# A tile of small scalars is declared 8 columns wide in place of 16, and all that lies behind it in SBUF starts 32 bytes earlier

## The reference

```
first block:  h = rms_norm(x)*(1+scale)+shift ; split(h @ w_in)
              window attention with context keys  +  gated delta rule in 64-token chunks, both directions
              x += gate * ((sigmoid*attn + sigmoid*delta) @ w_out)
              x += gate * (square(relu(h2 @ w_mlp1)) @ w_mlp2)
second block, twice:
              u, q, k, v = split(modulate(rms_norm(x)) @ w_in2)
              centred means of u over 2, 4, 8, 16 tokens, each group through a 128x128 matrix (w_pool)
              differential attention over context + latent keys
              x += gate * (mix @ w_out2) ;  x += gate * (square(relu(h2 @ w_m1)) @ w_m2)
              (the context stream likewise, in the first of the two layers only)
final rms_norm
```

## The kernel before

| tile | start before | rest by 64 |
|---|---|---|
| raw | 16512 | 0 |
| ws | 65664 | 0 |
| hh | 90240 | 0 |
| xT | 123008 | 0 |
| rs | 149056 | 0 |
| sq | 151104 | 0 |
| mi | 155200 | 0 |
| ar, ar2, hc1, gg, g2 | 155264 | 0 |
| yy, gc2 | 188032 | 0 |
| hc2 | 204416 | 0 |
| ctx2 | 220800 | 0 |

## Time and profile before

### The profile page before, as it was taken

The page is one execution under the profiler, slowest core; times in us unless marked ns, Lnnn a source line. Parts: engine busy times, 40 slices in busy tenths (PEclk is TensorE's granted clock), DMA queues, the critical chain, the costliest instruction groups (busy, mean ns, idle before and its releaser), DMA issues.

```text
span 2666.4 us, 45804 instructions
## 1 busy us (share of the span) xinstructions
PE 2505.2 (94%) x19622; PEld 2041.3 (77%) x19622; DVE 1557.0 (58%) x2412; ACT 931.7 (35%) x1599; POOL 115.6 (4%) x222
## 2 busy tenths in 40 slices
PE   6999977779999999999998999999999998999997
PEld 3777666667887788887777888888887766788886
DVE  3355577766666788854675556645445466544444
ACT  3344443323235223342553432222233254423322
POOL 0000001111100001000000000000000000000000
PEclk8999999989999999999999999999999999999999
DMA  6000000004653555411002123333321101222210
GB/s 278 32 32 1 33 3 4 4 4 166 222 210 129 178 193 190 174 44 59 5 32 80 64 95 127 127 127 127 127 95 44 64 32 65 94 101 115 100 64 32
DMA packets 32202, 244.88 MB, mean 92 GB/s; under 512 B 3616, under 2 KB 3776, under 8 KB 20992
## 3 DMA queue, kind: packets, MB, share of 16 engines
q1 hardware_dynamic: 11808, 164.83, 15.5%
q0 software_dynamic: 20192, 77.11, 9.1%
HBM read 239.83 MB, written 2.10 MB: 91 GB/s over the span
## 4 chain that ended last, share of the span: by engine, by line
PE 85%; DVE 9%; issue 3%; ACT 2%; DMA 1%; POOL 0%; DVEq 0%; ACTq 0%; POOLq 0%
PE ps L337 56%; PE ps L2190 2%; PE ps L2419 2%; PE ps L949 1%; PE ps L2447 1%; PE ps L2463 1%; PE ps L1370 1%; PE ps L367 1%; PE ps L905 1%; PE ps L2465 1%; PE ps L2464 1%; PE ps L369 1%; PE ps L368 1%; PE ps L950 1%; PE ps L951 1%
## 5 line engine op out<-in xcount | busy, mean ns | idle before, releaser
L337 PE MATMUL ps<-hh,ws 128*128 128x512 f32 x3216 | 751.7, 393 | 11.2 <-DVE hh L524 7.5
L337 PEld LDWEIGHTS ps<-hh,ws 128*128 128x128 f32 x3216 | 601.2, 188 | 143.9 <-issue 15.6
L318 ACT ACTIVATE ws<-raw 128x1024 fp32r<-128x1024 f32 x295 | 308.7, 1049 | 423.9 <-PE ps L337 390.8
L326 DVE TENSOR_TENSOR ws<-raw,ws 128x1024 fp32r<-128x1024 f32 x295 | 359.7, 1221 | 156.4 <-ACT ws L318 156.4
L337 PE MATMUL ps<-g,ws 128*128 128x512 f32 x1536 | 355.3, 390 | 0.0
L337 PEld LDWEIGHTS ps<-g,ws 128*128 128x128 f32 x1536 | 286.4, 188 | 58.0
L337 PE MATMUL ps<-gg,ws 128*128 128x512 f32 x960 | 221.5, 391 | 2.1 <-ACT ws L318 2.1
L1807 DVE SCALAR_TENSOR_TENSOR xT<-ps,mods,xT 128x512 f32<-128x512 f32 x120 | 90.0, 750 | 213.6 <-PE ps L337 206.3
L337 PEld LDWEIGHTS ps<-gg,ws 128*128 128x128 f32 x960 | 181.2, 189 | 40.6 <-ACT ws L318 2.4
L1970 DVE TENSOR_TENSOR sq<-sq 128x512 f32<-128x512 f32 (+1 forms) x128 | 80.0, 625 | 142.9 <-ACT sq L1947 142.9
L1947 ACT ACTIVATE sq<-ps 128x512 f32<-128x512 f32 (+1 forms) x128 | 69.3, 542 | 258.3 <-PE ps L337 244.3
(11 more groups left out here) (378 smaller groups left out, 3571.4 us busy)
## 6 DMA issues: line engine op xcount, KB each, us to landing
raw<-in_w_m SPq DMA_DIRECT2D x32, 2048.0 KB, 7.8
raw<-in_w_ada POOLq DMA_DIRECT2D x80, 512.0 KB, 3.9
raw<-in_w_mlp SPq DMA_DIRECT2D x16, 2048.0 KB, 7.9
ar<-in_w_ada POOLq DMA_DIRECT2D x48, 512.0 KB, 3.9
raw<-in_w_in SPq DMA_DIRECT2D x8, 2048.0 KB, 7.7
raw<-in_w_mg SPq DMA_DIRECT2D x8, 1536.0 KB, 7.2
raw<-in_w_out SPq DMA_DIRECT2D x6, 2048.0 KB, 8.0
raw<-in_w SPq DMA_DIRECT2D x5, 2048.0 KB, 7.9
```

The lines of the kernel that those rows point to most:

```text
L318: e.activation(w_of(n)[0], pieces[n][2], ACT.Copy).then_inc(*hi(n))
L326: e.tensor_tensor(l, pieces[n][2], h.bitcast(F32), ALU.subtract).then_inc(*lo(n))
L337: m = e.matmul(o, a, b, start=n == 0, stop=n == 3 * kt - 1)
```

## The change

The tile `mi` gets 8 columns in place of 16, 32 bytes in place of 64. Nothing else in the file is different.

```
--- before.py
+++ after.py
@@ -132,7 +132,7 @@
         ones = sb("ones", [P, P])
         rs = sb("rs", [P, T])
         sq = sb("sq", [P, 2, T])
-        mi = sb("mi", [P, 16])
+        mi = sb("mi", [P, 8])
         REST = 18432
```

## The result

The changed kernel is slower: its median is 2681.56 us (2679.49 to 2684.59, four runs), that of before in the same comparison 2666.86 us. The ratio is 1.0054, 95% interval 1.0040 to 1.0068, so 14.4 us with 10.7 to 18.1. I had forecast no change and called a loss 27 in 100 likely; the loss lies inside my range of 2658 to 2700 us and outside the forecast's own range.

What follows compares the result with a forecast made beforehand. The prediction took TensorE's matmuls to bound the kernel. All terms were 0, so 2668.16 us stayed 2668.16, or 2665.5 us on the median's scale; the range was 2658 to 2700 us, the forecast's own 2661 to 2671.

Steps and rivals of the forecast that it cites:

- Which engine the time hangs on: Whole kernel: TensorE, busy 2505.2 of 2666.4 us and 85% of the chain, so whatever stretches matmuls moves the time.
- The exchange rate: 5040 matmuls reading the region: they sit on the path nearly one for one, 1 ns more each being 5.04 us.
- I take 0 ns for each matmul: fp32r matmuls whose moving operand lies in the region, mostly line 337: no cost from a start with a rest of 32.
- The bound of 1 ns: Same matmuls: flights of the float32 pool matmuls leave 1 ns either way, -5 to +5 us.
- The look at group 3 of line 2211: Check after the change: this float32 pool pair, then starting on a multiple of 64, should still take 1.02 us.
- The fp32r rival: Matmuls on the region: an uneven start needs one more 64-byte block, 6.7 ns each, 33.6 us, 2699 us; chance 0.17.
- half a block: Matmuls on the region: half the extra 64-byte block, 3.4 ns each, giving 2682 us.
- the small things: ScalarE's and VectorE's writes, small matmuls' weight loads and DMA: about 16 us in full, 2682 us, half likelier; chance 0.10.
- The faster rival: Weights and moving tile on the same rest hinder each other; 32 bytes apart saves 33 us, 2633 us; chance 0.11.
- VectorE, ScalarE and DMA: Their accesses to the region: 0 each; bounds of 2 us, about 2.5 us and 2.9 us.
- Weights loaded from the region: Some 2,600 small matmuls loading weights from hc and ar: 0, with at most 9 us up or down.
- The two rules: SBUF's 16-byte cachelines make a 32-byte shift free; DMA fetching from 256-byte boundaries gives ar's loads 131 beats, not 132.

Runs made afterwards that it cites:

- e2: Kernel before with 32 bytes put ahead of ws and 32 behind it, so ws starts with a rest of 32: 2692.42 us, ratio 1.0102.
- e6: Kernel before with only the second block's g2, gc2, hc2 and ctx2 moved 32 bytes later: 2671.96 us, ratio 1.0007.
- m4: New kernel with line 337's matmul pattern alone, in plain float32 and fp32r at other widths and distances; float32 at 512 columns, 32 bytes: 41.36 us.
- e1: Kernel before with a 32-byte tile put ahead of raw, so every large tile starts with a rest of 32: 2665.98 us, ratio 1.0005.
- e5: Changed kernel with 32-byte gaps putting g2, gc2, hc2 and ctx2 back where they were: 2673.34 us, ratio 1.0018 against before.
- m1: New kernel with line 337's matmuls alone, weights and moving tile at varied starts: 227.5 ns with both on 64, 233.5 with only the moving tile off.
- the sweep: New kernel with line 337's matmuls alone, moving operand at growing distances from one weights tile; 227 ns at multiples of 256 bytes, 512 columns.

## Why the prediction was wrong

*Which engine the time hangs on* was right. The exchange rate was, too, for the change and for e2: the busy time added on the big products (15.6 and 28 us) came out in the time (14.4 and 27). In e6 it did not quite.

*TensorE, fp32r: "I take 0 ns for each matmul"* is the step that failed. Measured: +6.7 ns at 512 columns in an uninterrupted stretch and about -1.3 ns at 256. In busy time `g` +9.1, `gg` +6.1, `yy` +1.3, line 2190 on `hc` +0.5, `hc` -0.4 and `gc` -1.0 are 15.6 us, against 14.4 us (10.7 to 18.1) in the runs. What decides is the distance in bytes between the weights and the moving operand: it was a multiple of 256 and is now 32 bytes off.

The 0 came from float32 rows, of which I had written that they run at half the rate and may hide what fp32r can't. m4 shows just that: float32 is flat to 0.1 ns a matmul at every distance. The bound of 1 ns that I drew from their flights, and with it the chance of 0.62, was therefore a bound on another instruction. The text named the weakness but gave the rival that rests on it no more than 0.17. The look at group 3 of line 2211 in the changed kernel could not have shown the effect either: `w_pool` lies in `ar2` as well, so the weights moved along with the latent means. Only its two context tiles in `raw` stayed, and these, whose distance to their weights did change by 32 bytes, kept their 380 ns, as float32 does in m4.

*The fp32r rival* gave 6.7 ns and foretold 233 ns on `g` beside 227 on `hh`, which is what the profile shows. Its mechanism was wrong nonetheless: it is no extra block, since e1, with every start on a rest of 32, is as fast as before. And at 256 columns it foretold 127 ns where 118.7 came. Its 33.6 us (33.8 with the rounded 6.7 ns) are 2688 matmuls at 512 columns x 6.7 = 18.0 us, of which 16.5 are there in busy time, and 2352 at 256 columns x 6.7 = 15.8 us, which aren't. The range held the measured time because it had been stretched to reach this rival, and the 2682 us that the prediction names twice, for half a block and for the small things, are near it by luck: neither is what happened.

*The faster rival* looked at the right quantity, where the weights and the moving operand lie relative to each other, with the wrong sign at 512 columns. It was taken for unlikely because the pool matmuls were no faster at another distance, and these were float32.

*VectorE, ScalarE and DMA* were each priced at 0 and stayed there: 692 and 742 ns, 633 ns, 3.9 us. e1 confirms it for the kernel as a whole, and e5 for `ar` and `ar2`. *Weights loaded from the region* were priced at 0, too. Where the product is fp32r they follow the same distance, with the roles swapped: line 2190, with its weights in `hc` and `ws` moving, went from 23.9 to 24.4 us over 96 matmuls. That is 0.5 us, well inside the 9 us that I had allowed.

*The two rules.* m1 takes 231.7 ns at a distance of 16 bytes and 229.1 at 64 against 227 at 0. The Trainium skill, "SBUF — State Buffer", section Specifications, has 16-byte cachelines; by them, shifts of whole lines would cost nothing, and here they do, so I was wrong to let the rule speak against a loss. The rule on the loads' beats changed nothing that shows. What I had not weighed is the row on TensorE in the section Who interferes with whom of the same page: it gives TensorE two SBUF read ports, one for the moving operand and one for the load of weights, "independent", and the section adds that it never waits on anyone. The trace fits badly with "independent": with the same moving tile, moving the weights alone by 32 bytes takes the stream from 227.5 to 233.4 ns in m1. Where the wait arises, no run shows.

## What to carry to other kernels

Between two builds with the same instructions, the place of the tiles is a variable: give the moving tiles and the tile of weights one distance modulo 256 bytes and keep it when a small tile ahead of them grows or shrinks; declaring the large tiles first would do that, though no run here tried it. Here 0 was best at 512 columns of fp32r and not at 256, so the distance is to be measured for the width in use, and in the order of the real kernel, since the stream before counts. And a bound that comes from a slower instruction bounds only that instruction; where the operation in question runs at twice the rate, the range and the chances must follow the operation.

## What the hardware showed that I had not expected

The spacing of fp32r matmuls depends on the distance between stationary and moving operand with a period of 256 bytes, 227 to 234 ns at 512 columns in steps of 32 bytes, and 238 ns at a distance of 4 bytes. It depends on what ran before: at 256 columns 113 or 118 ns at the same addresses. The width matters in no simple way: differences of at most 1 ns at 384, 320, 192 and 128 columns, of 2 ns at 256 in the sweep (118 to 120), and a gain of 6.6 ns at 448 for a distance of 64 bytes. Why the pattern is as it is stays open: the runs vary addresses, widths and the number of columns of weights, and show no conflict directly.
